# FFN input loop: the inner chunk made between the second group's sums, sent three loads later, fetched by ScalarE's queue

## The reference

```
h = x + 0.5 * swiglu(rmsnorm(h), ffn1_w_in, ffn1_w_out)
h = h + concat(rmsnorm(spatial gating), rmsnorm(stick-breaking attention)) @ w_mix_out
h = h + cross attention of rmsnorm(h) over 256 memory tokens
h = h + 0.5 * swiglu(rmsnorm(h), ffn2_w_in, ffn2_w_out)
out = rmsnorm(h)
swiglu(x, w_in, w_out): gate, up = split(x @ w_in); (silu(gate) * up) @ w_out
```

## Time and profile before

| | us |
|---|---|
| median of 3 runs | 2127.22 (2126.7 to 2127.55) |
| the profiled execution | 2129.56 |
| its span in the profile | 2127.5 |

### The profile page before, as it was taken

One profiled execution on the slowest core, in us unless ns is written; L12 is line 12 of the kernel. 1 busy time (PEld: TensorE's weight loads), 2 busy tenths in 40 slices (PEclk: granted clock), 3 DMA queues, 4 the chain that ended last, 5 costly groups with the idle time before them and its releaser, 6 DMA issues.

```text
span 2127.5 us, 27271 instructions
## 1 busy us (share of the span) xinstructions
PE 2106.6 (99%) x9405; PEld 1740.4 (82%) x9405; DVE 1534.0 (72%) x1647; ACT 1089.3 (51%) x1249; POOL 38.4 (2%) x50
## 2 busy tenths in 40 slices
PE   9999999999999999999999999999999999999998
PEld 7788888888888888888888888887887888888887
DVE  7999999984555576566565656569999999964444
ACT  6555555553444455456544545455555555543433
POOL 0000000000000031000000000000000000000000
PEclk9999999999999999999999999999999999999999
DMA  7676667776666676765587766575667767775554
GB/s 278 223 231 218 221 231 228 226 245 239 208 228 214 220 265 218 237 213 184 178 285 239 237 208 191 189 247 198 229 226 223 224 217 221 225 287 195 190 188 157
DMA packets 185317, 472.37 MB, mean 222 GB/s; under 512 B 17056, under 2 KB 67616, under 8 KB 185120
## 3 DMA queue, kind: packets, MB, share of 16 engines
q1 hardware_dynamic: 183088, 464.11, 66.1%
q0 software_dynamic: 1728, 6.82, 0.9%
q10 hardware_dynamic: 432, 0.53, 0.1%
HBM read 443.60 MB, written 27.79 MB: 222 GB/s over the span
## 4 chain that ended last, share of the span: by engine, by line
PE 60%; DVE 18%; DMA 11%; issue 8%; ACT 2%; DVEq 0%; SPq 0%; ACTq 0%; POOLq 0%; POOL 0%
PE acc L1869 18%; PE acc L1871 18%; PE acc L1872 18%; DMA raw<-in_ffn_w_in 11%; DVE w_lo L1186 9%; DVE t_raw L1312 2%; DVE raw L1310 2%; DVE t_raw L1309 2%; DVE stage L1293 1%; PE acc L1893 1%; PE acc L1892 1%; PE acc L1894 1%; DVE stage L1226 1%; ACT w_hi L727 1%; DVE shared L1348 0%
## 5 line engine op out<-in xcount | busy, mean ns | idle before, releaser
L1186 DVE TENSOR_TENSOR w_lo<-raw,w_hi 128x1024 fp32r<-128x1024 f32 x765 | 924.8, 1223 | 477.1 <-ACT w_hi L727 474.9
L727 ACT ACTIVATE w_hi<-raw 128x1024 fp32r<-128x1024 f32 x765 | 796.8, 1056 | 857.5 <-PE acc L1872 532.7
L1869 PE MATMUL acc<-w_hi,a_hi 128*128 128x512 f32 x744 | 290.3, 390 | 0.5 <-DVE w_lo L1186 0.5
L1872 PE MATMUL acc<-w_hi,a_lo 128*128 128x512 f32 x744 | 289.6, 389 | 0.0
L1871 PE MATMUL acc<-w_lo,a_hi 128*128 128x512 f32 x744 | 289.5, 389 | 0.0
L1869 PE MATMUL acc<-w_hi,b_hi 128*128 128x512 f32 x576 | 225.6, 392 | 0.0
L1871 PE MATMUL acc<-w_lo,b_hi 128*128 128x512 f32 x576 | 224.3, 389 | 0.0
L1872 PE MATMUL acc<-w_hi,b_lo 128*128 128x512 f32 x576 | 224.2, 389 | 0.0
L1892 PE MATMUL acc<-w_hi,a_hi 128*128 128x512 f32 x460 | 179.0, 389 | 0.0
L1893 PE MATMUL acc<-w_lo,a_hi 128*128 128x512 f32 x460 | 179.0, 389 | 0.0
L1892 PE MATMUL acc<-w_hi,b_hi 128*128 128x512 f32 x460 | 179.0, 389 | 0.0
(11 more groups left out here) (273 smaller groups left out, 2645.1 us busy)
## 6 DMA issues: line engine op xcount, KB each, us to landing
raw<-in_ffn_w_in SPq DMA_DIRECT2D x349, 512.0 KB, 4.2
raw<-in_ffn_w_out SPq DMA_DIRECT2D x176, 512.0 KB, 4.3
raw<-in_w_mix_in SPq DMA_DIRECT2D x80, 512.0 KB, 4.4
raw<-in_w_ckv SPq DMA_DIRECT2D x64, 512.0 KB, 4.3
memq<-bounce SPq DMA_DIRECT2D x196, 128.0 KB, 4.3
bounce<-stage SPq DMA_DIRECT2D x37, 512.0 KB, 3.1
raw<-in_w_mix_out SPq DMA_DIRECT2D x32, 512.0 KB, 4.5
raw<-in_w_cq SPq DMA_DIRECT2D x32, 512.0 KB, 4.3
```

The source lines that it names most:

```text
L727: eng.activation(w_hi[:, u % RING], raw[:, u % RING], ACT.Copy).then_inc(w_hi_done, 1)
L1186: eng.tensor_tensor(w_lo[:, u % RING], raw[:, u % RING], w_hi[:, u % RING].bitcast(f32), ALU.subtract).then_inc(w_lo_done, 1)
L1869: eng.matmul(dst, x_hi[:, rows], w_hi[:, slot, i], start=start and i == 0, stop=False)
L1872: last = eng.matmul(dst, x_lo[:, rows], w_hi[:, slot, i], start=False, stop=stop and i == UK - 1)
```

## The change

Five things are changed, all in the two FFN input products.

1. `hidden` is split in its two instructions; they no longer stand ahead of the second group's sums, but between them.
2. The send stands ahead of load 10 instead of load 7.
3. The fetch is taken off SP and written into ACT's program, behind the rounding of load 7. ACT waits for `sent` and issues the four DMAs.
4. `turn`, `fill_hi` and `fill_lo` move from around loads 10 and 11 to behind load 12.
5. In the first pairs the mixed blocks are made at p = 5, 7, 9 (first FFN) and 9, 11, 13 (second) instead of 10, 12, 14, the clearing of `shared` moves from p = 8 to p = 4, and a Silu of one column (`first_exp`, a small buffer) is issued at p = 14 or p = 6, so that its table is loaded there.

```diff
-SEND_AT = 7
-MIX_AT = [10, 12, 14][-FAST:]
-FETCH_AT = 10
+SEND_AT = 10
+X_MIX_AT = [5, 7, 9]
+H3_MIX_AT = [9, 11, 13]
...
-                        if p == FETCH_AT:
-                            fetch(number(TURNS, hid) - 1 + j, first=base == FFN1_IN)
...
+                def fetch_again(turn):
+                    eng.wait_ge(sent, 16 * turn + 16)
+                    if base != FFN1_IN:
+                        eng.wait_ge(turned, turn)
+                    for q in range(4):
+                        eng.dma_start(xs[32 * q:32 * q + 32],
+                                      bounce[bass.ds(turn, 1), :, q * P:(q + 1) * P].rearrange(
+                                          "a (b j) n -> j (a b) n", j=32)).then_inc(fetched, 16)
...
                         split(base, j, FAST_AT[s] + 2, PAIR)
-                        if s == FAST - 1:
-                            fill_hi(turned, number(TURNS, hid) + j, hid_dst, src=stage4)
                         split(base, j, FAST_AT[s] + 3, PAIR)
+                        if s == 1:
+                            fetch_again(number(TURNS, hid) - 1 + j)
...
                     eng.activation(copy_p1, sum_p1, ACT.Copy).then_inc(p1_copied, 1)
+                    fill_hi(turned, number(TURNS, hid) + j, hid_dst, src=stage4)
...
+                    if p == 14:
+                        eng.activation(first_exp[:], ones[:, 0:1], ACT.Silu)
...
                     eng.tensor_tensor(b12, b12, b11, ALU.add).then_inc(t1_done, 1)
+                    if s == 1:
+                        hidden(j - 1, 0)
                     eng.wait_ge(t1_done, count)
                     eng.tensor_tensor(t_raw[:, 1], b12, b22, ALU.add).then_inc(t2_done, 1)
+                    if s == 1:
+                        hidden(j - 1, 1)
...
                     for p in range(4 * FAST, PAIR - 3):
                         unit_lo(j, p)
+                    turn(number(TURNS, hid) - 1 + j, stage4)
                     eng.wait_ge(p1_copied, done)
                     eng.tensor_tensor(shared[:, 0], sum_p6, copy_p1, ALU.add).then_inc(p6_added, 1)
+                    fill_lo(split_number(hid) - 1 + j, lo, hi, src=stage4)
                     unit_lo(j, PAIR - 3)
```

More of the change, by code:

```diff
@@ L906, in first_pair_of_x @@
                         squares("x", q, h[:, :, q * CH:(q + 1) * CH])
-                    if p - 1 in MIX_AT:
-                        s = MIX_AT.index(p - 1)
+                    if p == 14:
+                        eng.activation(first_exp[:], ones[:, 0:1], ACT.Silu)
+                    if p - 1 in X_MIX_AT:
+                        s = X_MIX_AT.index(p - 1)
                         mix_parts_hi(FFN1_IN, s, a_hi, FIRST_PAIR.index((1, s)) + 1)
@@ L1136, in first_pair_of_h3 @@
                         turned_h3_hi(DC - 1)
-                    if p - 1 in MIX_AT:
-                        s = MIX_AT.index(p - 1)
+                    if p == 6:
+                        eng.activation(first_exp[:], ones[:, 0:1], ACT.Silu)
+                    if p - 1 in H3_MIX_AT:
+                        s = H3_MIX_AT.index(p - 1)
                         mix_parts_hi(FFN2_IN, s, b_hi, HEAD_PAIR.index((1, s)) + 1)
@@ L1286, in up_drained, with hidden @@
                     eng.tensor_tensor(shared[:], acc[:, NT:2 * NT], shared[:], ALU.subtract).then_inc(up_read, 1)
[L1288 to L1296, removed]
+                def hidden(j, t):
+                    if t == 0:
+                        eng.wait_ge(up_read, silus[base] + 1 + j)
+                        eng.wait_ge(silu_done, silus[base] + 1 + j)
+                    step = eng.scalar_tensor_tensor(
+                        out=stage[:, t], in0=shared[:, t], scalar=rstd[:, stat(rs), t:t + 1],
+                        in1=stage[:, t], op0=ALU.mult, op1=ALU.mult)
+                    if t == NT - 1:
+                        step.then_inc(hid_done, 1)
                 def weight_sums(j, s):
@@ L1333, in pair @@
                         fast_lo(j, s)
-                        if s == FAST - 1:
-                            turn(number(TURNS, hid) - 1 + j, stage4)
                         unit_lo(j, FAST_AT[s] + 2)
@@ L1338, in pair @@
                             up_drained(j - 1)
-                        if s == FAST - 1:
-                            fill_lo(split_number(hid) - 1 + j, lo, hi, src=stage4)
                         unit_lo(j, FAST_AT[s] + 3)
-                        if s == 0:
-                            hidden(j - 1)
                     for p in range(4 * FAST, PAIR - 3):
                         unit_lo(j, p)
+                    turn(number(TURNS, hid) - 1 + j, stage4)
                     eng.wait_ge(p1_copied, done)
                     eng.tensor_tensor(shared[:, 0], sum_p6, copy_p1, ALU.add).then_inc(p6_added, 1)
+                    fill_lo(split_number(hid) - 1 + j, lo, hi, src=stage4)
                     unit_lo(j, PAIR - 3)
@@ L1353, in pair @@
                     eng.wait_ge(w_used, base + PAIR * j + GATE_END)
+                    eng.wait_ge(t_read, number(FILLS, hid) + j)
                     eng.tensor_tensor(stage[:, 0], acc[:, 0], copy_p1, ALU.add)
@@ L1366, in ffn_in @@
                 eng.sem_inc(gate_read, 1)
-                mixed = (a_hi, a_lo) if base == FFN1_IN else (b_hi, b_lo)
-                mix_parts_lo(base, MIX_AT.index(PAIR - 2), *mixed)
                 with eng.Fori(1, DC + 1) as j:
@@ L1381, in ffn_out @@
                     if u == 3:
-                        hidden[1](FJ - 1)
+                        hidden[1](FJ - 1, 0)
+                        hidden[1](FJ - 1, 1)
                     if u == U8:
@@ L1457, in first_pair_of_x @@
                         mean_square("x", DC, D)
[L1458 to L1462, removed]
+                    if p - 2 in X_MIX_AT:
+                        mix_parts_lo(FFN1_IN, X_MIX_AT.index(p - 2), a_hi, a_lo)
+                    if p in X_MIX_AT:
+                        mix_parts(X_MIX_AT.index(p), a_hi, a_lo)
+                    if p == 4:
                         chain(eng.memset(shared[:], 0.0))
@@ L1802, in first_pair_of_h3 @@
                                 GAIN_AT["ffn2_norm"] + 12)
[L1803 to L1807, removed]
+                    if p - 2 in H3_MIX_AT:
+                        mix_parts_lo(FFN2_IN, H3_MIX_AT.index(p - 2), b_hi, b_lo)
+                    if p in H3_MIX_AT:
+                        mix_parts(H3_MIX_AT.index(p), b_hi, b_lo)
+                    if p == 4:
                         chain(eng.memset(shared[:], 0.0))
```

## The result

| | before | changed |
|---|---|---|
| median, same chip | 2126.96 us (4 runs) | 2168.45 us (4 runs, 2165.88 to 2170.6) |
| the profiled execution | 2129.56 | 2167.72 |
| its span | 2127.5 | 2166.0 |

The account below looks back on a forecast made before the run. The loop was taken to be paced by DVE's work plus its wait for load 9. From 2129.6 us, +39 (loop) and -7 (passages) gave 2161.6, a forecast median of 2159 us, 1.5% slower; range 2120 to 2172.

Parts of the forecast that it names:

- B: Rival for the loop: ACT is held, but load 9 takes only 4.5 us; 2137 us, chance 0.15.
- C: Rival for the loop: ACT is not held and load 9 takes 5.6 us; about 2123 us, chance 0.08.
- Load 9, -0.2 us a pair: Loop: with the send behind it instead of the fetch, load 9 takes 5.6 us instead of 5.8; -0.2 us a pair.
- ACT held by the fetch, +1.8 us a pair: Loop: ACT waits for the send, then issues four DMAs, so `w_hi` of load 8 comes 1.8 us late.
- `hidden` between the sums, -0.24 us a pair: Loop: the split `hidden` fills two of DVE's waits between sums; -0.24 us a pair.
- Turn and fill later, +0.57 us a pair: Loop: one addition of 0.60 us covers ACT's `fill_hi`, so DVE waits longer ahead of `fill_lo`; +0.57 us a pair.
- Sum: Loop terms together: +1.9 us a pair, +39 us over 20 pairs.
- Passages, -7 us: First pairs into their loops: -5 us in the first FFN and -2 us in the second.
- What would show it: Trace signs: `w_hi` of load 8 some 3.3 us after load 9's landing; PE's `t_lo_part` waits 45 to 50 us.
- A: Rival: ACT issues everything before the sums are ready, load 9 takes 4.5 us, PE never waits; 2109 us, chance 0.10.
- that reading: Passages: with the skill's 1.38 us drain they would give 2 x 1.38 us more, some 2156 us; not followed.

Follow-up runs that it names:

- send8: The changed kernel with its send ahead of load 8 instead of load 10; 2132.14 us, ratio 0.9996 to the kernel before.
- send9: The changed kernel with its send ahead of load 9 instead of load 10; 2129.43 us, ratio 0.9988 to the kernel before.
- hidden_back: The changed kernel with `hidden` in one piece again, ahead of the second group's sums; 2172.91 us, ratio 1.0189 to the kernel before.
- turn_back: The changed kernel with `turn`, `fill_hi` and `fill_lo` back around loads 10 and 11; 2160.57 us, ratio 1.0131 to the kernel before.
- part5: The kernel before with part 5 of the change alone (mixed blocks, clearing of `shared`, early Silu); 2128.48 us, ratio 0.9982.
- fetch12: The kernel before with its fetch, still on SP, ahead of load 12 instead of load 10; 2130.14 us, ratio 0.9992.
- late12: The changed kernel with its send ahead of load 8 and its fetch issued by SP ahead of load 12, turn still late; 2129.61 us, ratio 0.9986.
- late11: The changed kernel with its send ahead of load 8 and its fetch issued by SP ahead of load 11, turn still late; 2116.41 us, ratio 0.9926.
- best: The changed kernel with send ahead of load 8, fetch on SP ahead of load 12, turn and fills back around loads 10 and 11; 2122.93 us, ratio 0.9954.

## Why the prediction came out right

The direction, the mechanism and the place were right; the forecast of 2159 us was 9 us low. That the time lies within 2120 to 2172 us says little by itself, since that range also held rivals B (2137 us) and C (2123 us); it is the rows that decide for the mechanism. By the prediction's own steps:

- *Load 9, -0.2 us a pair.* Right in kind and slightly too small. It took 5.4 us on the mean, not 5.6 (and 5.7 before, not 5.8), and DVE's wait ahead of the first sum fell from 2.08 to 1.74 us a pair (34.7 us, 20 times): -0.35.
- *ACT held by the fetch, +1.8 us a pair.* This is the term that was mis-sized. The send did land 1.3 us behind load 9. The four issues were taken from SP's 1.96 us; in the changed kernel they take 1.9 to 2.8 us (mean 2.3), with single issues up to 1.00 us, and end at +3.7 us on the mean. `w_hi` of load 8 starts another 0.2 us later, at +4.0 instead of +3.3, and DVE's gap is 2.24 us. In send8 and send9, where they go out at another moment, the same four take 1.83 to 1.98 us. Why they are slower here I did not test. In the changed kernel loads 10 and 11 are under way then and DVE makes the sums, but in send8 a load is under way and DVE is busy as well, so neither alone explains it. The prediction's lower end for this term has a slip: four issues of 0.33 us give +1.1, not +1.2; nothing hangs on it. That the issues stand behind a landed send and ahead of `w_hi` is the cause, and that is shown: with the send earlier the whole loss goes.
- *`hidden` between the sums, -0.24 us a pair.* Not contradicted, not settled (hidden_back).
- *Turn and fill later, +0.57 us a pair.* The gap ahead of `fill_lo` is 0.79 us where it was 0.27: +0.52, 10 us of the forecast's 11. turn_back took back 0.6%.
- *Sum.* -0.35 + 2.24 - 0.24 + 0.52 = 2.17 us a pair, 43 us; PE lost 45.6 us more in the loops. The forecast had 39.
- *Passages, -7 us.* The trace shows 6.8 us: PE's wait of 2.44 us is gone and the granted clock is 1.00. Measured by itself, part5 gave 4 us (1 to 7), so it is the trace of the changed kernel that bears out the 7, and not the times.
- *What would show it.* All were seen, with the sizes given above, but for one: PE's lateness was to show as waits for `t_lo_part` alone. It is split between `w_lo` of load 8 and `t_lo_part`; the sum, 46.4 us, is in the 45 to 50 that were forecast. The step that missed this had PE show all lateness of DVE at the third `t_lo_part`; but PE uses the `w_lo` of load 8 before that, and so waits for it first.
- The remaining difference comes from the runs themselves: the profiled execution before was 2.6 us above the median of 2126.96 us, that of the changed kernel 0.7 us below its own. Together with the 38.2 us between the two profiled executions that makes the 41.5 us measured.

*Rivals.* A (loop free) and C (ACT not held) needed ACT's issues to end before DVE's in-place sum; it ends 1.4 us behind load 9's landing, they end 2.0 to 2.9 us after it. C is what send9 then made: ACT not held and load 9 at 5.6 us, ratio 0.9988 (0.9975 to 1.0001) where C gave 2123 us, or 0.998. B needed load 9 at 4.5 us; one pair of 20 had less than 5 us. That a DMA close behind load 9 costs it about a microsecond is shown by fetch12, where the load without one took 4.5 us on the mean, against 5.7 with the fetch behind it and 5.4 with the send.

On the rule of the Trainium skill that SP's and ACT's DMAs share the 16 DMA engines (DMA: Bandwidth & Descriptors, "Issuing engines are not separate DMA queues"): send8 agrees with it. The fetch went out on ACT's queue, and load 9, on SP's, took 5.9 us in the pair shown and 6.1 on the mean, against 4.5 in fetch12 with nothing close behind it. On the drain of 1.38 us (ScalarE: Activation LUTs, "What ACT_TABLE_LOAD costs"): in the changed kernel, too, the small Silu starts 0.01 us behind the table load's end, and the load itself starts 0.02 us behind the rounding before it, so the trace shows no drain on either side. The passages gave 6.8 us, not the 9.8 of that reading:

```profile
40.19 1.04 ACT L725 ACTIVATE w_hi<-raw 128x1024 fp32r<-128x1024 f32 x1
41.25 1.28 ACT L917 ACT_TABLE_LOAD   x1
42.54 0.20 ACT L917 ACTIVATE first_exp<-ones 128x1 f32<-128x1 f32 x1
```

## What to carry to other kernels

A DMA that waits for another DMA should be issued by an engine whose next work is not wanted soon: the issues cost little, but their wait holds everything written behind them. So read two moments from the trace, when the awaited transfer lands and when the engine's next work is released. Only what the landing and the issues take beyond that release is paid: in send9 the issues ended before it and cost nothing, in the changed kernel they ended 2.0 to 2.9 us behind it and cost 2.24 us a pair.

A transfer on the queue has three prices that move against each other: the load ahead of it, its own reader, and the load behind it. Read all three gaps before moving one of them. fetch12 freed the load ahead and paid at the reader, late12 freed the reader and paid at the load behind, and late11, with the fetch one load earlier than either, gained 0.7% over before, of which part 5 by itself had given 0.2%.

## What the runs showed of the hardware

- A 512 KB send issued 0.53 to 0.59 us behind a 512 KB load landed 1.26 to 1.35 us behind it in all 80 pairs of four kernels (the changed kernel, turn_back, hidden_back, send9), whether the load took 4.0 or 6.3 us. Issued 3.1 us behind the load, as in send8, it landed 1.25 to 1.87 us behind it.
- Four DMA issues on ACT took 1.83 to 1.98 us in send8 and send9, but 1.9 to 2.8 us in the changed kernel; one alone took 0.32 to 1.00 us there, and the first of the four never more than 0.35.
- Load 9 took 3.7 to 4.8 us with nothing close behind it (best; mean 4.3), 5.4 on the mean with a send behind it (the changed kernel), 5.7 (4.4 to 6.6) with a fetch behind it on its own queue (before), and 6.1 (4.7 to 7.0) with the fetch on the other engine's queue during the load (send8).
- With the fetch issued 3.4 to 3.8 us behind load 9's issue, 0.4 to 1.3 us before it lands, load 9 took 3.8 to 4.7 us in 19 of 20 pairs (late11).
- An `ACT_TABLE_LOAD` took 1.28 us, with 0.02 us of idle time ahead of it and 0.01 us behind it (the changed kernel, at 41.25 us).
